# Four of the six modulation vectors computed in the stage of heads instead of the stage of modulation

## The chip, the cores and the metric

The kernel runs on one core of a Trainium2 chip. The metric is the device time of one execution in microseconds (us); lower is better. All data are float32.

## The reference, cut to what matters

The program is one block (two-way gated recurrence, convolution, attention, a layer of retrieved experts) followed by a second block of two layers. What concerns this change are the modulation vectors: two condition vectors, `c` and `c_ctx`, give six vectors of 1024 numbers each.

```python
sil_c, sil_cc = jax.nn.silu(c), jax.nn.silu(c_ctx)
mx = (sil_c @ w_ada[l] + b_ada[l])[:, None, :]
mc = sil_cc @ w_ada[l] + b_ada[l]
xsh1, xsc1, xg1, xsh2, xsc2, xg2 = jnp.split(mx, 6, axis=-1)
csh1, csc1, cg1, csh2, csc2, cg2 = jnp.split(mc, 6, axis=-1)
px = _split_in(_modulate(x, xsh1, xsc1) @ w_in[l])      # x * (1 + scale) + shift
pc = _split_in(_modulate(ctx, csh1, csc1) @ w_in[l])
...                                                     # 8 heads, convolution, attention, merge
x = _layer_norm(ALPHA * x + xg1 * mix_x, ln1_g[l], ln1_b[l])
x = _layer_norm(ALPHA * x + xg2 * _peer(_modulate(x, xsh2, xsc2), ...), ln2_g[l], ln2_b[l])
```

The projections of the heads need the first two vectors. The other four are used only after the attention, in the merge and the experts.

## The kernel before

Activations are kept transposed: 128 channels on the partitions, 8 blocks of channels, 512 tokens (256 context tokens) along the free dimension. Weights come as tiles of 128 output channels by all 1024 inputs, 512 KB each, loaded by SP into a ring of slots. SP waits, before a load, until TensorE has used up what was in the slot (`free_at`, counted on `filled`), TensorE waits for a tile's landing (`landed_at`). SP's loads go out in program order. A float32 matmul instruction appears as two records in the profile.

**Stage of modulation** (`phase_modulation`, L509). A ring of 8 slots, six rounds of 8 tiles of `w_ada`. For each tile TensorE does 8 matmuls (L562) with two columns, the silu of the two condition vectors, as the stationary operand and 128 weight columns as the moving one; the result is 2 rows by 128. Four tiles fill a bank, which ScalarE copies into `rows` (L548), 12 copies in all. When all six vectors are there, 48 transposes (L568) turn the rows into columns, VectorE adds the bias (L578) and adds one to the two scale vectors (L582), then scales and shifts x and the context (L586, L588) and converts masks (L590). ScalarE's queue loads x, the context, the constants and masks beside the weights. A stage ends with a barrier of all engines, and the next begins with GpSimd counting up each semaphore once and a second barrier.

**Stage of heads** (`phase_heads`, L598). Eight heads one after the other; a loop runs over the first seven, the eighth is written out. A head has seven weight tiles in a ring of seven and nine fills of PSUM banks (`fill`): 0 and 1 the convolution's inputs, 2 to 4 the gates, 5 the query, 6 and 7 the values of tokens and context, 8 the output gate. Fill n goes to bank n % 4 of banks 0 to 3, and waits for ScalarE's evacuation of what was there (`proj_out`).

TensorE's `body` of head i does fills 6, 7, 8 of head i; then, for the levels 0 to 6, waits for VectorE's products of the level (`qk_ready`, L966), makes two banks of scores (16 records, L734, banks 4 to 7) and, from level 1 on, fill level-1 of head i+1 (L687); then the scores of the diagonal (L744), of levels 8 and 7, of the context, and the output of the head (L779 to L785). The last head has no following fills.

VectorE per level: three taps of the convolution (L916), running sums of logarithms (L941, L950), products (L966), and from level 1 on two masked copies of the scores of the level before (L928), which wait for TensorE. ScalarE per level: four exponentials (`grow`, L840), released by VectorE's sums of the level before. SP loads tiles 5 and 6 of head i and then tiles 0 to 4 of head i+1, each as soon as its slot is free, which is nearly a head ahead of its use.

Of the kernel before, what the change touches and what calls it, by code (L numbers as in the profile page):

```python
# [16 lines left out]
P = 128  # L17
# [494 lines left out]
def phase_modulation(nc, io, mem):  # L512
# [4 lines left out]
    with Phase(nc, "mod") as ph:  # L517
        w = ph.stream(8, [(6, 8, list(range(8)))])
        B = ph.banks()
        cond, sil = ph.sb("cond", [P, DB, 2]), ph.sb("sil", [P, DB, 2])  # L520
        masks = ph.sb("masks", [P, N_MASKS, P])
        rows = ph.sb("rows", [2, 6 * D])
# [6 lines left out]
        @block.sync  # L529
        def _(sp):  # L530
            with sp.Fori(0, 6) as i:
                for k in range(8):
                    load_tile(sp, w, 0, k, i, io["w_ada"][i, k])

        @block.scalar
        def _(act):
            act.dma_start(cond[:], io["cond"]).then_inc(loaded, 16)
            act.dma_start(mem.par[:], io["params"]).then_inc(loaded, 16)
            act.dma_start(mem.con[:], io["consts"]).then_inc(x_loaded, 16)
            act.dma_start(mem.xT[:], io["x"]).then_inc(x_loaded, 16)  # L540
            act.dma_start(mem.cmT[:], io["ctx"]).then_inc(x_loaded, 16)
            act.dma_start(masks[:], io["masks"]).then_inc(x_loaded, 16)
            act.wait_ge(loaded, START + 32)
            nc.scalar.activation(sil[:], cond[:], ACT.Silu).then_inc(sil_ready, 1)
            with act.Fori(0, 6) as i:
                for half in range(2):
                    act.wait_ge(w.filled, w.fill_at(0, (half + 1) * PER_BANK - 1, i))
                    nc.scalar.activation(rows[:, bass.ds(i * D + half * 512, 512)], B[half][0:2, :],  # L548
                                         ACT.Copy).then_inc(row_out, 1)

        @block.tensor
        def _(pe):
            pe.wait_ge(sil_ready, START + 1)
            with pe.Fori(0, 6) as i:
# [10 lines left out]
            pe.wait_ge(row_out, START + CREDIT + 12)  # L565
            pe.wait_ge(x_loaded, START + 64)
            for m in range(48):
                last = nc.tensor.transpose(B[2][:, 2 * m:2 * m + 2], rows[:, m * P:(m + 1) * P],  # L568
                                           mem.c("ident")[0:2, 0:2])
# [3 lines left out]
        def _(dve):  # L573
# [3 lines left out]
            bias = mem.par[:, PARAM_AT["b_ada"]].unsqueeze(2).to_broadcast([P, 48, 2])  # L577
            seq(nc.vector.tensor_tensor(out=mem.mod[:], in0=B[2][:, 0:96].rearrange("p (m c) -> p m c", c=2),  # L578
                                        in1=bias, op=ALU.add))

            parts = mem.mod[:].rearrange("p (h q b) c -> p h q (b c)", h=2, q=3)
            seq(nc.vector.tensor_scalar_add(parts[:, :, 1, :], parts[:, :, 1, :], 1.0))  # L582
# [16 lines left out]
def phase_heads(nc, io, mem):  # L599
# [21 lines left out]
    with Phase(nc, "hd") as ph:  # L621

        w = ph.stream(RING, [(1, AHEAD, [0, 1, 4, 4, 5]), (HEADS - 1, F, [1, 2, 3, 4, 7, 7, 8]),
                             (1, F - AHEAD, [1, 2])])

# [32 lines left out]
        conv_read, tapped = sem("conv_read"), sem("tapped")  # L658
        block = ph.block(w)

        @block.sync
        def _(sp):
            def load(t, head):
                load_tile(sp, w, *place(t, head), io["w_head"][head, t])

            for t in range(5):
                load(t, 0)
            with sp.Fori(0, HEADS - 1) as i:
                for t in (5, 6):
                    load(t, i)  # L670
                for t in range(5):
                    load(t, i + 1)
            for t in (5, 6):
                load(t, HEADS - 1)

        @block.tensor
        def _(pe):
# [39 lines left out]
            def body(i, more):  # L717
                for n in range(AHEAD, F):
                    fill(n, i)

# [3 lines left out]
                for level in range(IN_CHUNK):  # L724
                    pe.wait_ge(qk_ready, START + i * (LEVELS + 2) + level + 1)
                    for dr in range(2):
                        if n < 4:
# [8 lines left out]
                        n += 1  # L736
                    if more and level > 0:
                        fill(level - 1, i + 1)
# [55 lines left out]
        def _(act):  # L794
# [28 lines left out]
            def body(i, more):  # L823
# [7 lines left out]
                for level in range(LEVELS):  # L831
# [10 lines left out]
                    ins.then_inc(grown, 1)  # L842
                    if more and level == 5:
# [39 lines left out]
        def _(dve):  # L883
# [104 lines left out]
            dve.wait_ge(tapped, START + HEADS * TAPS)  # L988

# [1925 lines left out]
class Memory:  # L2915


    def __init__(self, nc, ctx):
# [4 lines left out]
        self.mod = sb("modulation", [P, 48, 2])  # L2923
        self.xT = sb("xT", [P, DB, T])
# [190 lines left out]
```

## Time and profile before

| | |
|---|---|
| median of 3 runs | 5145.26 us (5143.11 to 5145.98) |
| the profiled execution | 5142.65 us |
| its span, first to last instruction | 5140.9 us |
| mean granted TensorE clock | 0.949 |
| TensorE busy | 4583.3 us, 89% of the span |
| VectorE, ScalarE busy | 54%, 34% |
| stage of modulation | from the start to 113.7 us |
| stage of heads | 117.65 (first load) to 1002.7 us |

Times in the profile count from the first instruction of the span. In a timeline a line gives the start, the time from the first to the last of the merged instructions, the engine (PE is TensorE's matmuls, PEld its weight loads, DVE VectorE, ACT ScalarE, SPq the queue of SP), the source line, what is written and read, and in brackets the idle time before it with the instruction that ended it. PEclk is the share of full speed that TensorE's clock was granted: 0.5 is 1.2 GHz and 1.0 is 2.4 GHz. Matmul ends are modelled, so the next start says more than an end does.

### The profile page before, as it was taken

Reading aid. Unit: us, or ns where it says so; the run is one execution under the profiler, and the core shown is the slowest. Engines: PE = TensorE matmul, PEld = TensorE weight load, DVE = VectorE, ACT = ScalarE, POOL = GpSimd, SP = SyncE. Lnnn points to the kernel's source line nnn. Section 1 sums busy time; section 2 is a strip of 40 time slices with the busy share of each in tenths; the row PEclk is TensorE's granted clock in tenths of the full one; section 3 lists DMA queues with packets and bytes.
Section 4 is the critical chain, followed back from the end, with each engine's and each line's share of the span. In section 5 each row is a group of like instructions: output and inputs, shape, how many; then the busy total and the mean of one; then the engine's idle time right before and its main releaser. Section 6 shows DMA issues by size and latency. Waiting matters only on the chain. (4 is left out here: it accounts for less than half of the span.)

```text
span 5140.9 us, 60695 instructions
## 1 busy us (share of the span) xinstructions
PE 4583.3 (89%) x21819; PEld 3657.5 (71%) x21819; DVE 2766.2 (54%) x5003; ACT 1741.5 (34%) x2490; POOL 412.8 (8%) x308
## 2 busy tenths in 40 slices
PE   7988888588899856699999999698999999999998
PEld 5555555344587425699999999576778877678787
DVE  0557775522334599788888887434343333444332
ACT  0243333223432103333333332336432233452322
POOL 0000000000000160122222222000000000000000
PEclk8999999799999979899999999899999999999999
DMA  6100110000122102678777875221222321113222
GB/s 259 58 29 29 37 37 21 21 28 16 41 94 93 49 19 123 228 274 282 272 274 276 280 274 200 70 70 44 73 92 96 95 86 62 50 62 98 89 95 84
DMA packets 195766, 575.47 MB, mean 112 GB/s; under 512 B 17312, under 2 KB 66720, under 8 KB 194336
## 3 DMA queue, kind: packets, MB, share of 16 engines
q1 hardware_dynamic: 157888, 433.77, 24.4%
q0 software_dynamic: 36864, 134.23, 7.7%
q10 hardware_dynamic: 864, 5.45, 0.3%
q8 instruction: 95, 1.56, 0.1%
q14 instruction: 55, 0.45, 0.0%
HBM read 546.13 MB, written 27.26 MB: 112 GB/s over the span
## 5 line engine op out<-in xcount | busy, mean ns | idle before, releaser
L402 DVE TENSOR_TENSOR tile_rest<-tile_raw,tile_up 128x1024 fp32r<-128x1024 f32 (+2 forms) x288 | 338.7, 1181 | 781.0 <-ACT tile_up L393 780.9
L410 PE MATMUL layer_psum<-hn_up,tile_up 128*128 128x512 f32 x1344 | 534.7, 398 | 21.2 <-DVE hn_rest L497 21.2
L411 PE MATMUL layer_psum<-hn_up,tile_rest 128*128 128x512 f32 x1344 | 527.0, 392 | 0.0
L412 PE MATMUL layer_psum<-hn_rest,tile_up 128*128 128x512 f32 x1344 | 526.7, 392 | 0.0
L393 ACT ACTIVATE tile_up<-tile_raw 128x1024 fp32r<-128x1024 f32 (+2 forms) x288 | 291.4, 1017 | 368.8 <-PE layer_psum L412 368.4
L687 PE MATMUL hd_psum<-xmT,hd_w 128*128 128x512 f32 x768 | 341.5, 599 | 15.7 <-DMA hd_w<-in_w_head 15.7
L1896 PE MATMUL ex_psum<-ex_t_up,ex_u_up 128*128 128x384 f32 x1024 | 344.2, 336 | 10.7 <-ACT ex_prod L1970 6.3
L1914 PE MATMUL ex_psum<-ex_prod_up,ex_v_up 128*128 128x384 f32 x1024 | 342.8, 335 | 3.8 <-DVE xT L2036 3.8
L1897 PE MATMUL ex_psum<-ex_t_up,ex_u_rest 128*128 128x384 f32 x1024 | 343.9, 336 | 0.0
L1898 PE MATMUL ex_psum<-ex_t_rest,ex_u_up 128*128 128x384 f32 x1024 | 343.7, 336 | 0.0
L1915 PE MATMUL ex_psum<-ex_prod_up,ex_v_rest 128*128 128x384 f32 x1024 | 342.6, 335 | 0.0
L1916 PE MATMUL ex_psum<-ex_prod_rest,ex_v_up 128*128 128x384 f32 x1024 | 342.6, 335 | 0.0
L410 PEld LDWEIGHTS layer_psum<-hn_up,tile_up 128*128 128x128 f32 x1344 | 255.2, 190 | 81.7 <-issue 29.7
L411 PEld LDWEIGHTS layer_psum<-hn_up,tile_rest 128*128 128x128 f32 x1344 | 255.1, 190 | 53.9 <-issue 1.9
L412 PEld LDWEIGHTS layer_psum<-hn_rest,tile_up 128*128 128x128 f32 x1344 | 254.7, 189 | 53.9
L687 PEld LDWEIGHTS hd_psum<-xmT,hd_w 128*128 128x128 f32 x768 | 144.6, 193 | 180.6 <-issue 180.6
L1962 ACT ACTIVATE ex_v_up<-tT 128x1024 fp32r<-128x1024 f32 x128 | 128.7, 1052 | 305.4 <-PE ex_psum L1916 301.7
L734 PE MATMUL hd_psum<-hd_qk 128*128 128x128 f32 x896 | 139.0, 320 | 91.3 <-DVE hd_qk L966 91.3
L734 PEld LDWEIGHTS hd_psum<-hd_qk 128*128 128x128 f32 x896 | 133.4, 232 | 115.2 <-issue 68.1
L1896 PEld LDWEIGHTS ex_psum<-ex_t_up,ex_u_up 128*128 128x128 f32 x1024 | 193.7, 189 | 11.4 <-issue 11.4
L1914 PEld LDWEIGHTS ex_psum<-ex_prod_up,ex_v_up 128*128 128x128 f32 x1024 | 192.7, 188 | 4.2 <-DVE xT L2036 4.2
L2036 DVE SCALAR_TENSOR_TENSOR xT<-ex_psum,modulation,xT 128x384 f32<-128x384 f32 x256 | 156.8, 612 | 71.7 <-PE ex_psum L1916 71.7
(415 smaller groups left out, 9532.8 us busy)
## 6 DMA issues: line engine op xcount, KB each, us to landing
ex_u<-in_peer_u SPq DMA_DIRECT2D x128, 512.0 KB, 6.7
tT<-in_peer_v SPq DMA_DIRECT2D x128, 512.0 KB, 7.2
tile_raw<-in_w_gu SPq DMA_DIRECT2D x88, 512.0 KB, 3.3
hd_w<-in_w_head SPq DMA_DIRECT2D x56, 512.0 KB, 3.9
mod_w<-in_w_ada SPq DMA_DIRECT2D x48, 512.0 KB, 4.9
mg_w_raw<-in_w_merge SPq DMA_DIRECT2D x48, 512.0 KB, 3.3
expert_table<-et_rows SPq DMA_DIRECT2D x6, 4096.0 KB, 11.7
ex_rows<-expert_table SPq DMA_DIRECT2D x64, 384.0 KB, 7.9
```

The source lines that it names most:

```text
L393: self.nc.scalar.activation(self.up[:, n % self.SLOTS, 0:blocks, :], self.raw[n % self.RAWS][:, 0:blocks, :], ACT.Copy).then_inc(self.up_r ...
L402: self.nc.vector.tensor_tensor(out=self.rest[:, n % self.SLOTS, 0:blocks, :], in0=self.raw[n % self.RAWS][:, 0:blocks, :], in1=self.up[:, ...
L410: self.nc.tensor.matmul(dst, w_up, up, start=first, stop=False)
L411: self.nc.tensor.matmul(dst, w_rest, up, start=False, stop=False)
L412: return self.nc.tensor.matmul(dst, w_up, rest, start=False, stop=last)
L687: last = nc.tensor.matmul(dst, weights[:, d, :], rhs[:, d, :], start=d == 0, stop=d == DB - 1)
L1896: nc.tensor.matmul(dst, u_up[par, t][:, d, :], t_up[:, d, :], start=d == 0, stop=False)
L1897: nc.tensor.matmul(dst, u_rest[par, t][:, d, :], t_up[:, d, :], start=False, stop=False)
L1898: last = nc.tensor.matmul(dst, u_up[par, t][:, d, :], t_rest[:, d, :], start=False, stop=d == DB - 1)
L1914: nc.tensor.matmul(dst, v_up[par, t][:, m, :], prod_up[par, t][:], start=first, stop=False)
L1915: nc.tensor.matmul(dst, v_rest[par, t][:, m, :], prod_up[par, t][:], start=False, stop=False)
L1916: last = nc.tensor.matmul(dst, v_up[par, t][:, m, :], prod_rest[par, t][:], start=False, stop=final)
```

## The change

The stage of modulation computes only the first two vectors: two rounds of 8 tiles, 4 copies, 16 transposes, its loops written out. The other 32 tiles are computed in the stage of heads, four in each head, from a ring of two slots of their own (`wm`), loaded by SP between tiles 5, 6 of head i and tiles 0 to 4 of head i+1. TensorE multiplies them behind fill 8 into bank 1, ScalarE copies the two rows after the exponentials of level 1, TensorE makes four transposes behind the scores of level 2 into bank 3, ScalarE copies those into `mem.mod` after the exponentials of level 3. Bias and the one are added at the stage's end. The silu vectors are kept in memory that outlives the stage.

```diff
@@ phase_modulation @@
-        w = ph.stream(8, [(6, 8, list(range(8)))])
+        w = ph.stream(8, [(2, 8, list(range(8)))])
...
-            with sp.Fori(0, 6) as i:
+            for i in range(2):
...
-            pe.wait_ge(row_out, START + CREDIT + 12)
+            pe.wait_ge(row_out, START + CREDIT + 4)
             pe.wait_ge(x_loaded, START + 64)
-            for m in range(48):
+            for m in range(16):
...
-            bias = mem.par[:, PARAM_AT["b_ada"]].unsqueeze(2).to_broadcast([P, 48, 2])
+            bias = mem.par[:, PARAM_AT["b_ada"]][:, 0:16].unsqueeze(2).to_broadcast([P, 16, 2])
...
@@ phase_heads @@
+        wm = Stream(ph, 2, [(HEADS, 4, [0, 1, 2, 3])], name="wm")
...
+        mod_row, mod_rows_out, mod_turned, mod_out, mod_done = (sb("mod_row", [2, 4 * P]), sem("mod_rows_out"),
+                                                                sem("mod_turned"), sem("mod_out"), sem("mod_done"))
+        w.credited.append(wm.filled)
         block = ph.block(w)
+        mod_tiles = io["w_ada"][2:6].rearrange("q (g k) p d n -> (q g) k p d n", k=4)
@@ sync @@
+            def load_mod(head):
+                for k in range(4):
+                    load_tile(sp, wm, 0, k, head, mod_tiles[head, k])
             for t in range(5):
                 load(t, 0)
             with sp.Fori(0, HEADS - 1) as i:
                 for t in (5, 6):
                     load(t, i)
+                load_mod(i)
                 for t in range(5):
                     load(t, i + 1)
             for t in (5, 6):
                 load(t, HEADS - 1)
+            load_mod(HEADS - 1)
@@ tensor, body(i, more) @@
                 for n in range(AHEAD, F):
                     fill(n, i)
+                pe.wait_ge(proj_out, START + i * F + 6)
+                for k in range(4):
+                    pe.wait_ge(wm.landed[k % 2], wm.landed_at(0, k, i))
+                    for d in range(DB):
+                        last = nc.tensor.matmul(B[1][0:2, k * P:(k + 1) * P], mem.sil[:, d, :],
+                                                wm.ring[k % 2][:, d, :], start=d == 0, stop=d == DB - 1)
+                    last.then_inc(wm.filled, 1)
...
                     for dr in range(2):
+                        if (level, dr) == (2, 1):
+                            pe.wait_ge(mod_rows_out, START + i + 1)
+                            pe.wait_ge(proj_out, START + i * F + 8)
...
+                    if level == 2:
+                        for m in range(4):
+                            last = nc.tensor.transpose(B[3][:, 2 * m:2 * m + 2], mod_row[:, m * P:(m + 1) * P],
+                                                       mem.c("ident")[0:2, 0:2])
+                        last.then_inc(mod_turned, 1)
                     if more and level > 0:
+                        if level == 4:
+                            pe.wait_ge(mod_out, START + i + 1)
                         fill(level - 1, i + 1)
@@ scalar, body, behind the exponentials of a level @@
+                    if level == 1:
+                        act.wait_ge(wm.filled, wm.fill_at(0, 3, i))
+                        act.wait_ge(mod_turned, START + i)
+                        nc.scalar.activation(mod_row[:], B[1][0:2, :], ACT.Copy).then_inc(mod_rows_out, 1)
+                    if level == 3:
+                        act.wait_ge(mod_turned, START + i + 1)
+                        nc.scalar.activation(mem.mod[:, bass.ds(i * 4 + 2 * DB, 4), :].rearrange("p m c -> p (m c)"),
+                                             B[3][:, 0:8], ACT.Copy).then_inc(mod_out, 1)
@@ vector, end of the stage @@
+            dve.wait_ge(mod_out, START + HEADS)
+            bias = mem.par[:, PARAM_AT["b_ada"]][:, 2 * DB:6 * DB].unsqueeze(2).to_broadcast([P, 4 * DB, 2])
+            nc.vector.tensor_tensor(out=mem.mod[:, 2 * DB:6 * DB, :], in0=mem.mod[:, 2 * DB:6 * DB, :], in1=bias,
+                                    op=ALU.add).then_inc(mod_done, 1)
+            dve.wait_ge(mod_done, START + 1)
+            nc.vector.tensor_scalar_add(mem.mod[:, 4 * DB:5 * DB, :], mem.mod[:, 4 * DB:5 * DB, :],
+                                        1.0).then_inc(mod_done, 1)
```

## Rows read from the trace of the kernel before

**Rows 1.** The page, section 1: busy time, share of the span, instructions.

```profile
PE 4583.3 (89%) x21819; PEld 3657.5 (71%) x21819; DVE 2766.2 (54%) x5003; ACT 1741.5 (34%) x2490; POOL 412.8 (8%) x308
```

**Rows 2.** Busy time by stretch: length, PE, PEld, DVE, ACT, POOL (instructions), PEclk, DMA share, GB/s.

```profile
25.00:102.00 77.00, 76.81 (x704) 59.59 (x701) 0.00 (x0) 6.38 (x12) 0.00 (x0) 1.00 0.79 286
...
281.07:386.00 104.93, 90.31 (x384) 58.77 (x383) 71.80 (x129) 39.97 (x72) 0.00 (x0) 0.93 0.10 35
386.00:489.29 103.29, 89.02 (x384) 57.76 (x383) 71.73 (x129) 39.97 (x72) 0.00 (x0) 0.95 0.10 36
```

**Rows 3.** Timeline of ScalarE in the stage of modulation: start, us, what. Copies 4 and 12.

```profile
46.04 0.59 ACT L548 ACTIVATE mod_rows<-mod_psum 2x512 f32 x1 [6.40 <-PE mod_psum L562]
...
101.94 0.59 ACT L548 ACTIVATE mod_rows<-mod_psum 2x512 f32 x1 [6.40 <-PE mod_psum L562]
```

**Rows 4.** Timeline of TensorE, head 2, between 386 and 462 us.

```profile
386.00 7.03 PE L687 MATMUL hd_psum<-xmT,hd_w 128*128 128x512 f32 x16
400.03 3.78 PE L734 MATMUL hd_psum<-hd_qk 128*128 128x128 f32 x16 [7.00 <-DVE hd_qk L966]
405.75 2.05 PE L734 MATMUL hd_psum<-hd_qk 128*128 128x128 f32 x16 [1.93 <-DVE hd_qk L966]
407.63 7.03 PE L687 MATMUL hd_psum<-xmT,hd_w 128*128 128x512 f32 x16
414.50 1.95 PE L734 MATMUL hd_psum<-hd_qk 128*128 128x128 f32 x16
...
461.40 1.66 PE L744 MATMUL hd_psum<-hd_q,hd_ksum 128*128 128x128 f32 x8 [3.42 <-DVE hd_ksum L973]
```

**Rows 5.** Timeline of VectorE, head 2: mask copies of level 1 and of level 7.

```profile
405.61 0.72 DVE L928 COPY_PREDICATED hd_sx<-masks,hd_psum 128x512 f32<-128x512 uint8 x1
...
450.45 0.73 DVE L928 COPY_PREDICATED hd_sx<-masks,hd_psum 128x512 f32<-128x512 uint8 x1 [1.06 <-PE hd_psum L734]
```

**Rows 6.** Timeline of all engines, end of the modulation stage, start of the heads.

```profile
102.58 3.19 PE L568 MATMUL mod_psum<-consts,mod_rows 2*128 2x2 f32 x48 [0.77 <-ACT mod_rows L548]
...
105.81 0.26 DVE L578 TENSOR_TENSOR modulation<-mod_psum,params 128x96 f32<-128x96 f32 x1 [105.81 <-PE mod_psum L568]
...
112.56 1.15 DVE L590 CAST masks<-mod_masks 128x1920 uint8<-128x1920 f32 x1
...
117.65 49.77 SPq L276 DMA_DIRECT2D hd_w<-in_w_head  x12
```

**Rows 7.** SP's loads; landing times: one alone (423.5), three queued with others (118.5 to 119.5).

```profile
414.86 44.69 SPq L276 DMA_DIRECT2D hd_w<-in_w_head  x7
...
DMA to landing us min/median/max: 3.2/3.2/3.2
...
DMA to landing us min/median/max: 5.9/6.8/7.5
```

**Rows 8.** Timeline of ScalarE, head 2: exponentials of levels 2 and 4.

```profile
404.47 0.42 ACT L840 ACTIVATE hd_grow<-hd_suf 128x256 f32<-128x256 f32 x1 [4.46 <-DVE hd_pre L950]
...
419.03 0.42 ACT L840 ACTIVATE hd_grow<-hd_suf 128x256 f32<-128x256 f32 x1 [5.94 <-DVE hd_pre L950]
```

**Rows 9.** Timeline of TensorE: scores and fills of heads 0, 3 and 7.

```profile
196.16 3.41 PE L734 MATMUL hd_psum<-hd_qk 128*128 128x128 f32 x16 [1.94 <-DVE hd_qk L966]
...
509.04 3.25 PE L734 MATMUL hd_psum<-hd_qk 128*128 128x128 f32 x16 [2.29 <-DVE hd_qk L966]
512.08 7.53 PE L687 MATMUL hd_psum<-xmT,hd_w 128*128 128x512 f32 x16
...
921.01 3.78 PE L734 MATMUL hd_psum<-hd_qk 128*128 128x128 f32 x16 [8.26 <-DVE hd_qk L966]
```

**Rows 10.** Busy time by stretch, as in rows 2: heads 2 and 3.

```profile
396.90:403.80 6.90, 3.77 (x16) 3.49 (x16) 6.54 (x14) 1.41 (x4) 0.00 (x0) 0.51 0.00 0
403.80:407.20 3.40, 1.47 (x14) 1.46 (x14) 3.25 (x9) 1.33 (x4) 0.00 (x0) 0.99 0.00 0
509.70:513.00 3.30, 3.30 (x15) 2.78 (x14) 2.94 (x5) 0.00 (x0) 0.00 (x0) 0.50 0.00 0
```

More of the change, by code:

```diff
@@ L517, in phase_modulation @@
     with Phase(nc, "mod") as ph:
-        w = ph.stream(8, [(6, 8, list(range(8)))])
+        w = ph.stream(8, [(2, 8, list(range(8)))])
         B = ph.banks()
-        cond, sil = ph.sb("cond", [P, DB, 2]), ph.sb("sil", [P, DB, 2])
+        cond, sil = ph.sb("cond", [P, DB, 2]), mem.sil
         masks = ph.sb("masks", [P, N_MASKS, P])
-        rows = ph.sb("rows", [2, 6 * D])
+        rows = ph.sb("rows", [2, 2 * D])
         row_out, turned = ph.sem("row_out"), ph.sem("turned")
@@ L544, in _ @@
             nc.scalar.activation(sil[:], cond[:], ACT.Silu).then_inc(sil_ready, 1)
-            with act.Fori(0, 6) as i:
+            for i in range(2):
                 for half in range(2):
                     act.wait_ge(w.filled, w.fill_at(0, (half + 1) * PER_BANK - 1, i))
-                    nc.scalar.activation(rows[:, bass.ds(i * D + half * 512, 512)], B[half][0:2, :],
+                    nc.scalar.activation(rows[:, i * D + half * 512:i * D + half * 512 + 512], B[half][0:2, :],
                                          ACT.Copy).then_inc(row_out, 1)
@@ L553, in _ @@
             pe.wait_ge(sil_ready, START + 1)
-            with pe.Fori(0, 6) as i:
+            for i in range(2):
                 for k in range(8):
@@ L576, in _ @@
             dve.wait_ge(turned, START + 1)
-            bias = mem.par[:, PARAM_AT["b_ada"]].unsqueeze(2).to_broadcast([P, 48, 2])
-            seq(nc.vector.tensor_tensor(out=mem.mod[:], in0=B[2][:, 0:96].rearrange("p (m c) -> p m c", c=2),
+            bias = mem.par[:, PARAM_AT["b_ada"]][:, 0:16].unsqueeze(2).to_broadcast([P, 16, 2])
+            seq(nc.vector.tensor_tensor(out=mem.mod[:, 0:16, :], in0=B[2][:, 0:32].rearrange("p (m c) -> p m c", c=2),
                                         in1=bias, op=ALU.add))
-            parts = mem.mod[:].rearrange("p (h q b) c -> p h q (b c)", h=2, q=3)
-            seq(nc.vector.tensor_scalar_add(parts[:, :, 1, :], parts[:, :, 1, :], 1.0))
+            seq(nc.vector.tensor_scalar_add(mem.mod[:, DB:2 * DB, :], mem.mod[:, DB:2 * DB, :], 1.0))
             seq.end(1)
@@ L988, in _ @@
             dve.wait_ge(tapped, START + HEADS * TAPS)
+            dve.wait_ge(mod_out, START + HEADS)
[5 more added lines that the diff above has]
+                                        1.0).then_inc(mod_done, 1)
+            dve.wait_ge(mod_done, START + 2)
 def phase_attention(nc, io, mem):
@@ L2923, in __init__ @@
         self.mod = sb("modulation", [P, 48, 2])
+        self.sil = sb("silu", [P, DB, 2])
         self.xT = sb("xT", [P, DB, T])
```

## The prediction

> **What bounds the kernel now.** I read the page first, then the busy time by stretch, then the timelines of ScalarE, TensorE and VectorE around the two stages that the diff touches. The page says that TensorE is busy for 89% of the span [rows 1], so any TensorE work that is taken off the path is worth its own time, and any that is put onto it costs that. Two places matter.
>
> The stage of modulation is nothing but TensorE: from 25 to 102 us it is busy 76.81 of 77 us, at full clock, while VectorE has no instruction at all [rows 2]. Its rhythm is to be seen in the copies that empty the banks, one for each four weight tiles: the fourth starts at 46.04 us, the twelfth and last at 101.94 [rows 3]. Nothing else can start before the end of this stage.
>
> In the stage of heads, TensorE and VectorE take turns as the bound. Take head 2 (386.00 to 489.29 us). TensorE ends the projection of the gate (fill 8) at 393.03 and then sits idle for 7.00 us until VectorE has made the first query and key products; then come the scores of level 0, 1.93 us of idle, and from 405.75 on it works without a gap (scores 1.95, a fill 7.03, again and again) until the fill of level 6 ends; then it waits 3.42 us for VectorE's key sum [rows 4]. In that gapless stretch TensorE is the slower of the two: at level 7 VectorE waits 1.06 us for the scores of level 6 [rows 5]. So a microsecond added to TensorE between 405.75 and 449 comes out at the end of the head, and one that fits into the 7.00 us does not. The last head has no fills of a following one, and VectorE alone paces it.
>
> **The change part by part.**
>
> 1. *Taken out of the stage of modulation: 32 of 48 tiles.* The first 16 are loaded and multiplied in the same order beside the same other transfers, so they end as now, with the fourth copy. What goes is the time from the fourth to the twelfth: 101.94 - 46.04 = 55.90 us [rows 3], that is 1.747 us for a tile. Of 48 transposes in 3.19 us 16 stay [rows 6]: 32 x 66 ns = 2.13 us. VectorE's bias add takes 0.26 us for 96 columns [rows 6]; for a third of the columns there, and half of them in the add of one, I take 0.1 us off. The rest (scaling x and the context, the masks) is unchanged. **-58.1 us**, all of it on the path; the ACT copies were beside it. The loop in these streams is written out, which I cost at nothing between instructions that already follow without a gap.
>
> 2. *The section of four tiles put into each head, after fill 8.* Its first wait (the evacuation of q) is met: ScalarE did that while the fill ran. The matmuls are the same as those taken out, 4 x 1.747 = 6.99 us, against 7.00 us of idle [rows 4]. But the ring has only two slots. Tile 2 can be loaded only when tile 0 is used up, at 393.03 + 1.75 = 394.8. From the end of a fill (407.63 + 7.03) to the issue of the load that it releases are 0.2 us [rows 4, 7], and a tile that travels alone lands 3.2 us after its issue [rows 7]: tile 2 is there at 398.3 and tile 3, released at 396.5, at 400.0, so tile 2 runs to 400.1 and tile 3 to 401.9. The scores of level 0, ready at 400.03, run from 401.9 to 403.8, where they end today too, since they take 3.78 us at the low clock and 1.95 at the full one [rows 4]. Level 1 isn't ready before 405.75, and VectorE's first mask copy begins at 405.61 [rows 5]. So this costs **0**, under a cover of about 1.9 us. Its bound upward: the last of five tiles queued together landed after 7.5 us [rows 7]; with that for tile 3 (404.3) level 1 begins at 408.0, 2.2 us late, or 15.4 us over the seven heads with fills. I take the value for a lone tile, since here SP has nothing else in flight when it sends tile 2 and only one tile when it sends tile 3.
>
> 3. *The queue of SP.* The five tiles of the next head stood ahead of nothing; now they stand behind the waits for tiles 0 and 1, and are sent only at about 397. Today they go a whole head ahead. With 3.2 to 7.5 us to land, the first is there by 404.5 and is used at 407.63, the others are used at steps of 8.65 us [rows 4, 7]: **0**, cover 3 us. In head 0 they go 9 us ahead of level 1, at about 187, for use at 199.6 [rows 9].
>
> 4. *Four transposes in level 2* stand in TensorE's gapless stretch: 4 x 66 ns = 0.27 us [rows 6], in seven heads **+1.9 us**. The waits ahead of them and ahead of fill 3 are for copies that ScalarE has long made. Should each hand-over cost another 0.15 us, it would be 1 us more.
>
> 5. *ScalarE.* It waits for the fourth tile (401.9) and copies two rows in 0.59 us [rows 3], ending at 402.6; its next exponentials start at 404.47, released by VectorE. After the exponentials of level 3 it waits for the transposes (TensorE reaches them at 414.50 + 1.95 + 0.27 = 416.7) and makes a copy smaller than 0.59 us; its next work starts at 419.03 [rows 4, 8]. **0**, covers of 1.9 and about 1.8 us. Were they gone, the exponentials of the next level would be late, and VectorE's next level behind them.
>
> 6. *The clock.* Heads 1, 3 and 5 take 104.93 us each and heads 2, 4 and 6 103.29 [rows 2]. The difference is in one spot: in head 3 the scores of level 1 take 3.25 us and the fill behind them 7.53, against 2.05 and 7.03 in head 2 [rows 4, 9]. After the 7.00 us of idle the granted clock is at 1.2 GHz (0.51 of full speed from 396.90 to 403.80); in head 2 it is at 2.4 GHz by level 1 (0.99 from 403.80 on). In head 3 it rises too, and falls again about the second idle, of 2.29 us (0.50 from 509.70 to 513.00) [rows 9, 10]. With the section in the long idle, TensorE comes to level 1 hardly rested: 3 x 1.64 = 4.9 us. Head 0 pays part of this too (scores of level 1 of 3.41 us [rows 9]): 1.4 us. **-6.3 us**; bounds: 0 if the slow spells only move, and some -13 if four of the low spells behind the 3.42 us of idle (eight matmuls in 1.66 us there, where sixteen take 1.95 [rows 4]) go as well, at about 1.7 us each, as that of head 3 costs.
>
> 7. *Ends of the stage.* Seven more semaphores and one credit are counted up before it. Between VectorE's last instruction at 113.71 and the first load at 117.65 lie 3.94 us with 31 such increments [rows 6]: at most 8 x 0.13 = 1.0 us, I take +0.5. Behind the last head, an add of the bias and an add of one with their two waits: I take 0.26 us for each add [rows 6] and 0.2 for the waits, **+0.7 us**.
>
> Sum: -58.1 + 0 + 0 + 1.9 + 0 - 6.3 + 0.5 + 0.7 = **-61.3 us**. The profiled execution took 5142.65 us (span 5140.9), 2.6 us under the median of 5145.26; I put the same sum on both: 5081.4 for such an execution, **5084.0 us for the median**.
>
> **The rivals.** (A) *The section doesn't fit its gap.* Either the tiles land late (part 2), or TensorE goes to 1.2 GHz at the pause between tile 1 and tile 2. The profile leaves it open: a pause of 1.93 us was followed by full clock and one of 2.29 by the low one [rows 4, 9, 10], and mine is estimated at 1.7 to 2.0. If the low clock held from tile 2 on, tiles 2 and 3 and the scores would take 3.5 + 3.5 + 3.8, to 409.1, 3.3 us past the 405.75: 23 us in seven heads, and the 6.3 us of part 6 are lost: 5084.0 + 23 + 6 = 5113. With late tiles alone it is 5099. For it: the ring of two. Against: a low spell shorter than the section costs only the 1.9 us of cover.
> The Trainium skill has a rule against this change ("TensorE: Matmul & The Clock Gate", section "HAM oscillation — how this bites in real kernels"): bursts of some 2 us of matmuls, each behind a wait for its own transfer of 3 to 5 us, run cold every time. By that rule the time would be this rival's upper case. The trace here agrees with it for a long idle and not for a pause under 2 us.
>
> (B) *The idle isn't usable*, and each head grows by the section: seven heads x 6.99 = 48.9 us, and no gain from the clock: 5084.0 + 48.9 + 6.3 = 5139, no change that counts. For it: TensorE is 89% busy. Against: the idle of 7.00 us ahead of level 0 stands in each of heads 0 to 6, and one of 8.26 in the last [rows 4, 9].
>
> (C) *Slower*: SP's queue. The next head's tiles stand behind the mod tiles; if fill 0 of the next head waited for its tile, all the gapless stretch would move. The change turns into a loss when each of seven heads loses over 61.3 / 7 = 8.8 us, so when the first tile lands after 407.63 + 8.8 = 416.4, 19 us after it was sent. At 22 us it would be 5167. Against: no tile of this stage took over 7.5 us [rows 7].
>
> (D) *More than forecast*: low spells at the ends of heads go too: 5077.
>
> **How the numbers follow.** Forecast 0.81, A 0.12, B 0.02, C 0.02, D 0.03. A difference of 0.2%, or 10 us, is about what a measurement of this kernel can tell from none. Forecast, A and D are faster by more (0.96), B is within it (0.02), C slower (0.02). The range takes in D, the bounds of parts 4, 6 and 7, and the half of A in which tiles only land late (5099 and a little behind it): 5075 to 5103.
>
> **What would show it.** The fourth and last copy of the stage of modulation at 46.0, the first head load at 60.0. In each head two pauses of the section, before tile 2 (about 1.8 us) and hardly one before tile 3; scores of level 0 in about 1.95 us; level 1 released by VectorE and not by the end of scores; heads of about 103.5 us, all alike. VectorE's wait at level 7 at 1.3 us. I would be wrong if level 1 began behind VectorE's release, if the low clock showed inside the section, if ScalarE's exponentials of levels 2 and 4 had TensorE as releaser, or if a wait on a head tile appeared ahead of fill 0.

## The result, and the profile after

Median of 4 runs 5081.24 us (5077.55 to 5084.41), against 5145.62 us (5143.11 to 5149.23) for the kernel before in the same comparison: ratio 0.9874, 95% interval 0.9857 to 0.9891. The difference is 64.4 us, the forecast was 61.3, and 5081.24 lies in the range given. The profiled execution took 5079.55 us, its span is 5077.8 us, 63.1 shorter than before.

The page of the changed kernel, section 1, share of the span by engine [rows 1]:

```profile
PE 4562.2 (90%) x21819; PEld 3635.3 (72%) x21819; DVE 2765.8 (54%) x5005; ACT 1742.9 (34%) x2498; POOL 411.9 (8%) x308
```

TensorE has the same 21819 records and is 21 us less busy, though nothing was taken from its work; the mean granted clock is 0.957 now and was 0.949. The scores of level 0 make 13 of the 21 us: they take 2.05 us in each head now and took 3.4 to 3.8 before. None of that reaches the time, as level 1 waits for VectorE in both kernels.

The end of the stage of modulation and the start of the heads in the changed kernel, timeline of all engines [rows 3, 6]:

```profile
44.51 0.59 ACT L548 ACTIVATE mod_rows<-mod_psum 2x512 f32<-2x512 f32 x1 [6.40 <-PE mod_psum L562]
...
45.15 1.16 PE L568 MATMUL mod_psum<-consts,mod_rows 2*128 2x2 f32 x16 [0.68 <-ACT mod_rows L548]
...
53.03 1.15 DVE L589 CAST masks<-mod_masks 128x1920 uint8<-128x1920 f32 x1
58.61 1.75 SPq L276 DMA_DIRECT2D hd_w<-in_w_head  x4
```

The fourth copy is the last. It starts at 44.51 us, 57.43 us ahead of the twelfth before. Sixteen transposes take 1.16 us. The first load of the heads goes out at 58.61, 59.04 us earlier than before.

Head 2 of the changed kernel, TensorE's timeline [rows 4], and for the end of a head also a line of head 3:

```profile
324.85 7.03 PE L699 MATMUL hd_psum<-xmT,hd_w 128*128 128x512 f32 x16
331.81 3.66 PE L736 MATMUL hd_psum<-hd_wm,silu 128*2 128x128 f32 x32
337.16 1.91 PE L736 MATMUL hd_psum<-hd_wm,silu 128*2 128x128 f32 x16 [1.69 <-DMA hd_wm<-in_w_ada]
339.60 1.91 PE L736 MATMUL hd_psum<-hd_wm,silu 128*2 128x128 f32 x16 [0.53 <-DMA hd_wm<-in_w_ada]
341.44 2.05 PE L756 MATMUL hd_psum<-hd_qk 128*128 128x128 f32 x16
344.62 2.05 PE L756 MATMUL hd_psum<-hd_qk 128*128 128x128 f32 x16 [1.13 <-DVE hd_qk L1003]
...
353.38 1.95 PE L756 MATMUL hd_psum<-hd_qk 128*128 128x128 f32 x16
355.26 0.40 PE L761 MATMUL hd_psum<-consts,hd_mod_row 2*128 2x2 f32 x4
...
362.56 1.95 PE L756 MATMUL hd_psum<-hd_qk 128*128 128x128 f32 x16
...
400.79 1.15 PE L773 MATMUL hd_psum<-hd_q,hd_ksum 128*128 128x128 f32 x8 [3.41 <-DVE hd_ksum L1010]
...
502.94 2.07 PE L773 MATMUL hd_psum<-hd_q,hd_ksum 128*128 128x128 f32 x8 [3.40 <-DVE hd_ksum L1010]
```

This is the predicted picture. Two tiles run at once; then 1.69 us of pause before tile 2 and 0.53 before tile 3. The scores of level 0 end at 343.5, and level 1 waits for VectorE (0.86 to 1.21 us in six of the seven heads with fills, and for nobody in head 5, where tile 3 came 1.50 us late). From the start of fill 8 to level 1 it is 19.77 us, as before (19.75): the section costs nothing there. But the four transposes aren't the 0.27 us of the forecast. From the scores of level 2 to those of level 3 it is now 9.18 us, and 8.65 to 8.69 at the levels behind it.

ScalarE in the same head: the two copies and the exponentials behind them, each still released by VectorE [rows 8]. Then VectorE's mask copy of level 7 [rows 5].

```profile
341.54 0.59 ACT L875 ACTIVATE hd_mod_row<-hd_psum 2x512 f32<-2x512 f32 x1 [2.64 <-PE hd_psum L736]
343.34 0.42 ACT L869 ACTIVATE hd_grow<-hd_suf 128x256 f32<-128x256 f32 x1 [1.21 <-DVE hd_pre L987]
...
355.80 0.18 ACT L878 ACTIVATE modulation<-hd_psum 128x8 f32 x1 [3.85 <-PE hd_psum L761]
357.90 0.42 ACT L869 ACTIVATE hd_grow<-hd_suf 128x256 f32<-128x256 f32 x1 [1.92 <-DVE hd_pre L987]
```

```profile
389.86 0.73 DVE L965 COPY_PREDICATED hd_sx<-masks,hd_psum 128x512 f32<-128x512 uint8 x1 [1.31 <-PE hd_psum L756]
```

The two copies take 0.59 and 0.18 us, and end 1.2 and 1.9 us ahead of the next exponentials. VectorE's wait at level 7 has grown from 1.06 to 1.31 us.

Busy time by stretch in the changed kernel, with the columns of [rows 2]: heads 2 and 3, then the 3.5 us behind VectorE's key sum in each of them.

```profile
324.85:427.01 102.16, 93.48 (x452) 60.35 (x451) 71.71 (x129) 40.79 (x74) 0.00 (x0) 1.00 0.16 56
427.01:531.85 104.84, 96.17 (x452) 62.53 (x451) 71.81 (x129) 40.79 (x74) 0.00 (x0) 0.97 0.15 55
400.80:404.40 3.60, 3.60 (x25) 3.39 (x26) 2.23 (x3) 1.19 (x2) 0.00 (x0) 1.00 0.00 0
502.90:506.40 3.50, 3.46 (x12) 3.20 (x13) 2.37 (x3) 0.00 (x0) 0.00 (x0) 0.50 0.00 0
```

Behind the 3.4 us of idle at the end of the head the clock is still at 2.4 GHz in head 2 and at 1.2 GHz in head 3. That is the whole difference between a head of 102.16 us and one of 104.84: the step from the diagonal's scores to those of the context takes 3.61 us in the one and 6.30 in the other.

Where the 63.1 us are, by the same points in both traces: to the last copy -57.4 us; from there to the first load of the heads -1.6; to fill 8 of head 0 nothing; the seven heads from there -4.2 (729.31 to 725.14); from fill 8 of head 7 to the first load of the attention +0.8, of which 0.3 are a slower end of that head at the low clock; all the rest -0.7.

### The profile page after: what moved, and what is told of

The parts are those of the page before. It is cut to its first block and busy times, and to the rows that moved or that the text cites. A ratio compares the mean times of both kernels' runs of the same rounds, so it can differ in the third digit from the quotient of the medians.

```text
span 5077.8 us, 60622 instructions
## 1 busy us (share of the span) xinstructions
PE 4562.2 (90%) x21819; PEld 3635.3 (72%) x21819; DVE 2765.8 (54%) x5005; ACT 1742.9 (34%) x2498; POOL 411.9 (8%) x308
## 5 line engine op out<-in xcount | busy, mean ns | idle before, releaser
L1942 PEld LDWEIGHTS ex_psum<-ex_t_up,ex_u_rest 128*128 128x128 f32 x1024 | 193.7, 189 | 0.0
L1943 PEld LDWEIGHTS ex_psum<-ex_t_rest,ex_u_up 128*128 128x128 f32 x1024 | 193.6, 189 | 0.0
```

Of the source, the lines that this page charges most:

```text
L1942: nc.tensor.matmul(dst, u_rest[par, t][:, d, :], t_up[:, d, :], start=False, stop=False)
L1943: last = nc.tensor.matmul(dst, u_up[par, t][:, d, :], t_rest[:, d, :], start=False, stop=d == DB - 1)
```

## The experiments

The totals of kernels scatter by some microseconds, so the stage is read from the traces, one execution of each kernel. The table has, for each kernel, the seven heads from fill 8 of head 0 to fill 8 of head 7; how many of them pay extra at level 1 (over 9 us from the scores of level 1 to those of level 2, where 8.76 is the full clock); the step from level 2 to level 3; and the sum over seven heads of the time from the diagonal's scores to those of the context, 3.61 us each at full clock. It is worked out from the timelines of TensorE.

```
kernel           seven heads  pay at level 1  step 2-3  ends of heads   median of runs
before               729.31        4            8.65        36.96        5145.62
changed              725.14        0            9.18        35.28        5081.24
filler_only          728.64        5            8.65        34.09        5140.5
filler_longer        725.02        0            8.65        38.82        5138.48
no_section           728.04        6            8.65        31.99        5088.0
no_pause             736.21        6            9.18        35.27        5093.28
turn_early           726.78        0            8.65        40.47        5079.22
warm_end             715.21        0            9.18        25.28        5074.28
warm_and_turn        711.49        0            8.65        25.26        5066.6
sp_loop              724.96        0            9.18        35.08        5084.95 (one run)
loads_swapped        725.38        0            9.18        35.49        5084.48 (one run)
```

**The heads without the new section.** What does the section cost or give, net? In `no_section` its loads, matmuls, transposes and copies are left out, and four of the six vectors hold the bias alone.

```diff
-                load_mod(i)
...
-                for k in range(4):
-                    pe.wait_ge(wm.landed[k % 2], wm.landed_at(0, k, i))
-                    ...
```

> The changed kernel with all the work on vectors 2 to 5 left out of the heads (no loads, matmuls, transposes or copies; those four vectors hold the bias alone). Theory (about 59 us come from the stage of modulation, and the section itself is worth some 4 us net by the clock): first head load at 58 to 60 us, heads 0 to 6 at 725 to 731 us, alternating between two lengths as before, the whole about 5087, slower than the changed kernel though it does less. Rival (the section costs something net): under 5081, heads 0 to 6 shorter than the 725.1 us of the changed kernel.

Measured: 5088.0 us (5082.32 to 5090.53), ratio to before 0.9886 (0.9869 to 0.9904), heads 728.04 us. The theory holds: the kernel that does less is slower than the changed one in the heads, by 2.9 us. It pays 10.0 us in six heads at level 1, saves the 3.7 us of the transposes, and its heads' ends happen to be 3.3 us cheaper. The totals alone don't show this: of the 8.0 us between the profiled executions 6.2 lie behind the heads. TensorE's timeline of head 2 shows the price at level 1: idle of 7.00 us, scores at the low clock, 1.94 us of idle, and low again.

```profile
337.26 3.77 PE L744 MATMUL hd_psum<-hd_qk 128*128 128x128 f32 x16 [7.00 <-DVE hd_qk L976]
342.98 3.74 PE L744 MATMUL hd_psum<-hd_qk 128*128 128x128 f32 x16 [1.94 <-DVE hd_qk L976]
```

**Is it the filled idle?** `filler_only` is the kernel before with matmuls that nobody needs behind fill 8, and no transfers.

```diff
+                pe.wait_ge(proj_out, START + i * F + 6)
+                for f in range(40):
+                    nc.tensor.matmul(B[1][0:2, 0:P], mem.xmT[:, f % DB, 0:2], mem.xmT[:, f % DB, 0:P],
+                                     start=True, stop=True)
```

> The kernel before, with 40 matmuls added in each head behind fill 8 (two columns stationary, 128 moving, no data used, no transfers): 8.7 us of TensorE work into the idle of 7.0 us plus the pause behind the level-0 scores. Theory (the heads got shorter because TensorE doesn't go to 1.2 GHz ahead of level 1): heads 0 to 6, 729.3 us before, come down to about 723, with full clock at level 1 in every head, give or take 5 us as the low spells at the heads' ends shift; the whole about 5139. Rival 1 (the clock has nothing to do with it, the gain came from the order of loads or from elsewhere): 729.3 us, 5145.6. Rival 2 (the idle can't be used): 729.3 + 7 x 1.7 = 741 us or more.

Measured: 5140.5 us median of 10 runs, ratio 0.9993 (0.9983 to 1.0002), heads 728.64 us. The theory as I had put it fell: the long idle is gone, and five heads of seven still pay at level 1. The heads are where rival 1 had them (729.3 us); that the total came near the 5139 us of the theory is chance. TensorE's timeline in head 3:

```profile
503.14 2.05 PE L736 MATMUL hd_psum<-hd_qk 128*128 128x128 f32 x16
507.14 2.58 PE L736 MATMUL hd_psum<-hd_qk 128*128 128x128 f32 x16 [1.94 <-DVE hd_qk L968]
509.51 8.22 PE L687 MATMUL hd_psum<-xmT,hd_w 128*128 128x512 f32 x16
```

The scores of level 0 run at full clock now, but 1.94 us of idle follow, and in the middle of the scores of level 1 the clock falls (2.58 us for sixteen records, then a fill of 8.22). So filling the 7 us ahead of level 0 isn't enough; the next guess is that the idle left right ahead of level 1 counts. `filler_longer` has 44 filler matmuls for 40, and nothing else.

> The kernel before with 44 filler matmuls in each head where filler_only had 40, so that the idle ahead of level 1 is 1.0 us, as in the changed kernel, and no longer 1.9. Theory (what counts is how long TensorE rests right ahead of level 1; with 1.9 us it still fell to 1.2 GHz in five heads of seven): no head pays the 1.65 us at level 1, and heads 0 to 6 take 722 to 726 us plus what the spells at the heads' ends make of it, the whole about 5139. Rival (the gain needs the pauses or the transfers of the section): two to five heads still pay at level 1, 728 us as in filler_only.

The same place in `filler_longer`:

```profile
506.37 2.05 PE L736 MATMUL hd_psum<-hd_qk 128*128 128x128 f32 x16 [1.06 <-DVE hd_qk L968]
508.26 7.03 PE L687 MATMUL hd_psum<-xmT,hd_w 128*128 128x512 f32 x16
```

With 1.06 us of idle, as in the changed kernel, no head pays, and the heads take 725.02 us; the median is 5138.48 us, ratio 0.9986 (0.9977 to 0.9996). The four penalties of before, 3 x 1.65 + 1.37 = 6.3 us, are all gone, and the ends of the heads, which fell to other places, took 1.9 of them. The gain needs neither the section's work nor its transfers. One thing isn't separated here: the four matmuls more both shorten the last idle and lengthen the work ahead of it.

**The pauses of the section.** If the remaining idle is what counts, the two pauses for tiles 2 and 3 should do good, by making level 0 late. `no_pause` takes them away without a third slot: tiles 2 and 3 aren't loaded, and tiles 0 and 1 are multiplied twice.

```diff
-                    pe.wait_ge(wm.landed[k % 2], wm.landed_at(0, k, i))
+                    if k < 2:
+                        pe.wait_ge(wm.landed[k], wm.landed_at(0, k, i))
```

> The changed kernel, with tiles 2 and 3 of each head's section neither loaded nor waited for (tiles 0 and 1 are multiplied twice, so the values are those of the wrong tiles): the same matmuls without the pauses of 1.7 and 0.7 us. Theory (the pauses cost nothing and even keep TensorE's idle ahead of level 1 short): idle ahead of level 1 grows from 1.0 to 3.4 us, in most heads the clock is at 1.2 GHz at level 1 again, and heads 0 to 6 take 728 to 738 us instead of 725.1. Rival (the pauses cost time, or nothing at all): 721 to 725 us.

TensorE's timeline in head 2:

```profile
334.32 7.15 PE L737 MATMUL hd_psum<-hd_wm,silu 128*2 128x128 f32 x64
341.41 2.05 PE L757 MATMUL hd_psum<-hd_qk 128*128 128x128 f32 x16
347.13 3.68 PE L757 MATMUL hd_psum<-hd_qk 128*128 128x128 f32 x16 [3.67 <-DVE hd_qk L1004]
350.63 7.05 PE L699 MATMUL hd_psum<-xmT,hd_w 128*128 128x512 f32 x16
```

Measured: 5093.28 us (5090.57 to 5095.25), ratio to before 0.9897 (0.9880 to 0.9913), heads 736.21 us. A section without waits is 11.1 us slower over seven heads than one with them: it ends 2.5 us earlier, level 1 comes no sooner, as VectorE releases it, and the 3.67 us of idle in between put TensorE at 1.2 GHz in six heads of seven (six penalties are 11.0 us). The ends of the heads cost the same in both. Here the matmuls are the same, and apart from the loads that are left out only the place of the rest differs. It isn't the sum of the rests: between fill 8 and level 1 of head 2 the changed kernel rests 1.69 + 0.53 + 1.13 = 3.35 us and pays nothing, `filler_only` rests 1.9 us in one piece and pays in five heads.

**What if the cover is gone?** `ring1` has one slot for the section's tiles (its index in TensorE's stream follows).

```diff
-        wm = Stream(ph, 2, [(HEADS, 4, [0, 1, 2, 3])], name="wm")
+        wm = Stream(ph, 1, [(HEADS, 4, [0, 1, 2, 3])], name="wm")
```

> The changed kernel with one slot instead of two for the modulation tiles, so that each of three tiles waits for its own transfer of 3.5 us. Theory: section 7.0 + 3 x 3.6 = 17.8 us, level 1 begins 7 to 9 us behind VectorE's release, which all comes out at the head's end: seven heads 725 + 49 to 63 us, the whole 5130 to 5145. Rival (by the rule of short bursts behind transfers, TensorE runs at 1.2 GHz in the section and behind it): 5.2 us more in each head, the whole 5165 to 5180.

One execution: 5169.36 us, heads 807.23 us. The section of head 2, timeline and then busy time by stretch:

```profile
353.35 1.91 PE L736 MATMUL hd_psum<-hd_wm,silu 128*2 128x128 f32 x16
358.70 2.97 PE L736 MATMUL hd_psum<-hd_wm,silu 128*2 128x128 f32 x16 [3.44 <-DMA hd_wm<-in_w_ada]
365.08 3.57 PE L736 MATMUL hd_psum<-hd_wm,silu 128*2 128x128 f32 x16 [3.42 <-DMA hd_wm<-in_w_ada]
372.48 3.57 PE L736 MATMUL hd_psum<-hd_wm,silu 128*2 128x128 f32 x16 [3.83 <-DMA hd_wm<-in_w_ada]
375.98 4.04 PE L756 MATMUL hd_psum<-hd_qk 128*128 128x128 f32 x32
```

```profile
353.30:358.70 5.40, 1.96 (x17) 1.28 (x17) 3.60 (x7) 3.26 (x6) 0.00 (x0) 1.00 0.28 97
358.70:376.00 17.30, 10.06 (x49) 5.40 (x49) 7.05 (x16) 1.43 (x4) 0.00 (x0) 0.52 0.43 152
```

The rival is what happened. Each of the last three tiles waits 3.4 to 3.8 us for its transfer, the clock is at 0.52 of full speed from 358.70 on, tiles 2 and 3 take 3.57 us and no longer 1.91, and level 1 begins 11.8 us behind VectorE's release. So what rival (A) of the prediction feared, the low clock inside the section, exists; its price can't be compared (11.7 us a head here, 3.3 us there), since `ring1` has three long waits and (A) one short one. Here the trace agrees with the rule of the Trainium skill ("TensorE: Matmul & The Clock Gate", section "HAM oscillation — how this bites in real kernels"), by which short bursts behind transfers of 3 to 5 us all run cold: tiles 2 and 3 do wholly, tile 1 in part (2.97 us). The pauses of the changed kernel's two-slot ring are shorter than those of the rule, 1.6 to 1.9 us before tile 2 and 0.4 to 1.5 before tile 3, and in all eight heads its section ran at 2.4 GHz, each tile in 1.91 us.

**The transposes.** `turn_early` moves the four transposes behind the scores of level 0.

```diff
-                        if (level, dr) == (2, 1):
+                        if (level, dr) == (0, 1):
...
-                    if level == 2:
+                    if level == 0:
```

> The changed kernel with the four transposes moved from behind the scores of level 2 to behind the scores of level 0, where TensorE rests 1.0 us. Theory (in level 2 they cost 0.53 us a head, since the step from its scores to those of level 3 is 9.18 us instead of 8.65): that step goes back to 8.65 us, 3.7 us less in seven heads, 3.2 where a head has no rest ahead of level 1; the whole about 5077.5, apart from 3 us either way by the low spells at the heads' ends. Rival (VectorE bounds the levels, so the step doesn't reach the end of the head): heads as long as now.

The step of level 2 is back at 8.65 us in all seven heads, so 3.7 us are really saved there. The heads as a whole take 726.78 us all the same, 1.6 more than the changed kernel, since the low spells at their ends cost 5.2 us more, which is beyond the 3 us that I had allowed. Head 1 shows a bad one in TensorE's timeline, 6.63 us for what takes 3.61:

```profile
294.46 2.07 PE L773 MATMUL hd_psum<-hd_q,hd_ksum 128*128 128x128 f32 x8 [3.42 <-DVE hd_ksum L1010]
...
301.09 3.17 PE L801 MATMUL hd_psum<-hd_full 128*128 128x512 f32 x7
```

The median, 5079.22 us (5072.79 to 5084.38), can't be told from that of the changed kernel.

**The ends of the heads.** `warm_end` puts 12 matmuls that nobody needs into the 3.4 us of idle ahead of the diagonal's scores, into a bank that is free then; `warm_and_turn` has this and the early transposes.

```diff
+                pe.wait_ge(masked, START + i * N_MASKS + 12)
+                for f in range(12):
+                    nc.tensor.matmul(B[7][0:2, 0:P], mem.sil[:, f % DB, :], mem.xmT[:, f % DB, 0:P],
+                                     start=True, stop=True)
                 pe.wait_ge(qk_ready, START + i * (LEVELS + 2) + LEVELS + 1)
```

> The changed kernel with 12 matmuls without use (two columns stationary, into a free bank) in the idle of 3.4 us ahead of the scores of the diagonal. Theory (that idle puts TensorE at 1.2 GHz behind it and costs 1.5 to 2.7 us in five heads of seven): the step from the diagonal's scores to those of the context is 3.61 us in heads 0 to 6, which together lose 10 us; the whole about 5071. Rival 1 (the low spells only move to level 1): the same total. Rival 2 (the filler is in the way): the idle turns into a late diagonal, heads as long or longer.

> Both of turn_early and warm_end. Theory: they add, as one acts on the gapless stretch and the other behind it: 13.5 us less than the changed kernel, 5067 us, and faster than both kernels compared. Rival: one takes away what the other gives, 5071 or more.

`warm_end`: 5074.28 us (5066.84 to 5076.53), ratio to before 0.9855 (0.9840 to 0.9870), heads 715.21 us, 9.9 us under the changed kernel. `warm_and_turn`: 5066.6 us (5064.58 to 5068.44), ratio 0.9843 (0.9829 to 0.9856), heads 711.49 us, 13.7 under it, against 13.5 expected. In both the seven ends cost 3.61 us each, and the 3.7 us between them are what the early transposes save: the rival of `turn_early` is refuted here. Head 2 of `warm_and_turn`, TensorE's timeline, and the stretch of the head:

```profile
337.41 2.06 PE L756 MATMUL hd_psum<-hd_qk 128*128 128x128 f32 x16
339.40 0.41 PE L761 MATMUL hd_psum<-consts,hd_mod_row 2*128 2x2 f32 x4
339.89 2.05 PE L756 MATMUL hd_psum<-hd_qk 128*128 128x128 f32 x16
...
348.65 1.95 PE L756 MATMUL hd_psum<-hd_qk 128*128 128x128 f32 x16
...
357.30 1.95 PE L756 MATMUL hd_psum<-hd_qk 128*128 128x128 f32 x16
...
392.05 2.78 PE L771 MATMUL hd_psum<-xmT,silu 128*2 128x128 f32 x24
395.53 1.15 PE L777 MATMUL hd_psum<-hd_q,hd_ksum 128*128 128x128 f32 x8 [0.70 <-DVE hd_ksum L1014]
...
399.14 3.60 PE L805 MATMUL hd_psum<-hd_full 128*128 128x512 f32 x8
```

```profile
320.12:421.76 101.64, 96.01 (x476) 62.28 (x475) 71.63 (x129) 40.67 (x74) 0.00 (x0) 1.00 0.16 57
```

All seven heads take 101.63 to 101.65 us at full clock, where there were lengths of 102.16 to 104.84. The eighth head shows that the fillers must stand right ahead of the scores. It has no fills that keep TensorE busy until then, so its 12 matmuls start at 889.52 us, and 11.24 us of idle follow. The clock is low behind it, 2.08 us for eight records and not 1.15 (TensorE's timeline of `warm_and_turn`):

```profile
903.79 2.08 PE L777 MATMUL hd_psum<-hd_q,hd_ksum 128*128 128x128 f32 x8 [11.24 <-DVE hd_ksum L1014]
```

The 14.6 us between the medians (5081.24 and 5066.6) are more than the spread of either: `warm_and_turn` is faster than both kernels compared.

**Two of SP's matters.** The fourth copy came 1.5 us sooner than forecast. `sp_loop` puts SP's 16 loads of the first stage back into a loop of two rounds and leaves the other streams written out; `loads_swapped` sends the next head's five tiles ahead of the section's four.

```diff
@@ sp_loop @@
-            for i in range(2):
+            with sp.Fori(0, 2) as i:
                 for k in range(8):
                     load_tile(sp, w, 0, k, i, io["w_ada"][i, k])
@@ loads_swapped @@
-                load_mod(i)
                 for t in range(5):
                     load(t, i + 1)
+                load_mod(i)
```

> The changed kernel with SP's loads of the stage of modulation in a loop of two rounds again, TensorE's and ScalarE's streams left written out. Theory (the written-out stream sends the first tiles sooner, in 0.47 us steps instead of 0.6, and so more of them ahead of ScalarE's large loads; that is why the first copy comes at 19.6 us and no longer at 24.9, and the fourth 1.5 us earlier): first copy near 25 us, fourth near 46. Rival (it is TensorE's or ScalarE's stream, or chance): the fourth copy at 44.5.

```profile
19.64 0.59 ACT L548 ACTIVATE mod_rows<-mod_psum 2x512 f32<-2x512 f32 x1 [11.16 <-PE mod_psum L562]
```

```profile
23.04 0.59 ACT L548 ACTIVATE mod_rows<-mod_psum 2x512 f32<-2x512 f32 x1 [15.91 <-PE mod_psum L562]
...
45.91 0.59 ACT L548 ACTIVATE mod_rows<-mod_psum 2x512 f32<-2x512 f32 x1 [6.40 <-PE mod_psum L562]
```

Above, in ScalarE's timeline, stands the first copy of the changed kernel, then the first and the fourth of `sp_loop`: first copy 23.0 instead of 19.6, fourth 45.9 instead of 44.5. In the eight kernels with a written-out stream, the changed one among them, the fourth is at 44.4 to 45.2, in the three with a loop of six at 46.0 to 46.9. The theory holds for the fourth copy, from one execution of each; the first came 2 us ahead of the 25 expected. The landings point the same way: tiles 1 to 3 land at 7.7, 11.5 and 17.7 us in the changed kernel and at 11.5, 17.4 and 21.1 before, and in `sp_loop` tiles 2 and 3 are back at 17.3 and 21.1. That the order of the queue among ScalarE's large loads is the mechanism was not tried by itself.

> The changed kernel with SP sending the five tiles of the next head ahead of the four of the section and no longer behind them. Theory (SP's order costs nothing, since the first tile of the next head has 3 us to spare, and may matter only by the pause before tile 3, which then travels alone): heads 0 to 6 within 3 us of the 725.1 of the changed kernel, no wait for a head tile in either, pause before tile 3 of 0.1 to 0.5 us. Rival (the wait behind the two slots delays the next head's tiles): heads shorter by over 3 us.

Heads 725.38 us, none waits for one of its own tiles: the order costs nothing, as forecast. Only the detail about tile 3 was wrong, with a pause of 0.91 us in head 2 (0.53 in the changed kernel) and 0.7 to 1.0 us in heads 1, 4, 5 and 6. The next head's tiles can't be the reason: in head 2 they were sent 40 us earlier, from 284.85 to 294.52, and had landed. What is in flight beside tile 3 is tile 2, sent 1.74 us before it. In the changed kernel, too, tile 2 lands 3.2 to 3.5 us after its issue and tile 3 after 3.8 to 5.1, over the eight heads. This is tile 3 of head 2, issued at 335.64:

```profile
DMA to landing us min/median/max: 3.9/3.9/3.9
```

In head 2 of `loads_swapped` it is 4.3 us, with nothing else of SP on its way. Why the second of the two takes longer is left open.

Head 3 of this run shows more: the low clock inside a two-slot section (TensorE's timeline).

```profile
442.08 5.32 PE L736 MATMUL hd_psum<-hd_wm,silu 128*2 128x128 f32 x32 [1.96 <-DMA hd_wm<-in_w_ada]
```

Behind a pause of 1.96 us tiles 2 and 3 take 5.32 us, where two warm tiles take 3.66. That is the low clock of rival (A). It ends within tile 3, and the scores of level 0 still begin 1.9 us ahead of level 1's release, so level 1 is on time and the head pays nothing for it.

## Why the prediction was right, point by point

1. *32 tiles out of the first stage.* The last copy moved by 57.43 us, the forecast was 55.90. The missing 1.5 us are the sentence that costed the written-out loop at nothing: it looked at TensorE's stream, where that is so, and not at SP's, which sends its first tiles sooner (`sp_loop`; the mechanism behind that is argued, not shown). Behind the last copy -1.6 us came, where the shares of parts 1 and 7 in it made -1.7.

2. *The section at no cost.* Right, with its pauses: 1.7 us forecast as 1.8 before tile 2, and 0.4 to 1.5 before tile 3, where I had hardly one. The forecast gave tile 3 the 3.2 us of a tile that travels alone; it took 3.8 to 5.1. In head 5 the cover of 1.9 us was used up to the last.

3. *SP's queue.* Right, no head waits for a tile of its own.

4. *The transposes.* Under-sized: 0.53 us a head instead of 0.27, 3.7 in seven heads instead of 1.9. The 66 ns are right for one in a row of 48; what I took at 0 to 0.15 us for each hand-over was 0.26 in all. `turn_early` shows that this cost goes away with the place.

5. *ScalarE.* Right.

6. *The clock.* The sum, -6.3 us, is what the level-1 penalties came to, and they are gone in all seven heads. But the reason in the prediction, that filling the 7 us lets TensorE come to level 1 "hardly rested", doesn't hold, and that the number came out is luck. By the prediction's own times (scores of level 0 to 403.8, level 1 at 405.75) 1.9 us of idle stay ahead of level 1, which is what `filler_only` has, with five penalties. What did it is that the last idle was cut to 1.2 us or less, and it was the transfers' pauses that cut it: I had counted the one before tile 2 as a danger and the one before tile 3 as hardly there. The reading behind rival (A), full clock behind a pause of 1.93 us and low behind 2.29, left out head 0, where a pause of 1.94 was followed by the low clock [rows 9]; in `no_section` 1.94 is followed by it in three heads. The ends of the heads gave another 1.7 us, inside the bound. That bound counted four low spells there where the trace of before has one in each of seven heads, 1.67 us each.

7. *Ends of the stage.* +0.8 us, forecast +0.7; 0.3 of the 0.8 are the clock at the end of the last head, which leaves about 0.5 for the adds and their waits.

The total is nearer than the terms. Against the forecast the first stage gave 1.4 us more, the ends of the heads 1.7 more and the stages behind 0.7 more, and the transposes took 1.8 back.

One sign of the prediction failed: the heads aren't "all alike" at 103.5 us. Their mean is 103.6, but they take from 102.16 to 104.84, as the clock at their ends goes.

Of the rivals, (A) is absent from the changed kernel, but by little: its longest pause before tile 2 is 1.94 us, and in `loads_swapped` one of 1.96 did bring the low clock into the section. There it cost nothing, by the very reason that the prediction gave against (A), that a short spell only uses up the cover. With one slot, in `ring1`, it cost much. (B) is refuted by the 19.77 us from fill 8 to level 1. (C) is refuted by the traces: no fill waited for a transfer; its 5167 us at a landing of 22 us should by its own working be about 5164. (D) came in a small part, and with `warm_end` in full.

## What to carry to other kernels

Work that is taken from a stage with one busy engine and put into an idle of the same engine in another stage is worth its full time, as long as the idle is really long enough with all that the work waits for: lay the pauses of its transfers into the gap, one after the other, before trusting it. Then ask what the moved work does to the idle that remains, since in these runs two or three short rests left TensorE's clock alone where a single one of 1.9 us often did not. A few matmuls without use, right ahead of the critical ones, can be worth more than the move's last details. And where effects of 1.7 us appear and vanish from head to head, compare the stages' parts and not the totals.

## What the runs showed that I had not expected

A section with waits was faster than the same section without them, by 11.1 us over seven heads (`no_pause`).

Idle of at most 1.3 us ahead of level 1 was never followed by the low clock there (49 heads of seven kernels: the changed one, `filler_longer`, `turn_early`, `warm_end`, `warm_and_turn`, `sp_loop` and `loads_swapped`), 1.9 to 2.3 us was in 15 of 21 heads (before, `filler_only`, `no_section`), and 3.7 us in six of seven. The pauses before tile 2 fit in. Of 45 of them under 1.9 us (eight heads of the six two-slot kernels with all loads) none was followed by the low clock, and of the three of 1.94 to 1.98 us one was, in `loads_swapped`. So in these traces the clock held behind every single idle of 1.88 us or less in this part of a head, and from 1.93 us on it fell in some heads and not in others. What decides there is not shown, and it isn't the length alone: in the kernel before 1.94 us is followed by the low clock in head 0 and 1.94 in heads 4 and 6 isn't.

The stages behind the heads, which no kernel here touches, took between 4123.6 and 4136.4 us from the first matmul of the attention to the end of the span in the profiled executions. I didn't follow this further. It is as large as the effects studied, and it is why medians were not used to weigh them.
